# Opening of the up-projection: the fourth right-form difference made by GpSimd instead of VectorE

## The reference, cut to what matters

```
def conv_gated_mlp(h, w_up, conv_w, conv_b, w_down):
    """Up-projection -> causal depthwise conv (3) -> GELU-gated product -> down-projection."""
    z = causal_depthwise_conv(h @ w_up, conv_w, conv_b)
    g, val = jnp.split(z, 2, axis=-1)
    return (jax.nn.gelu(g, approximate=False) * val) @ w_down
```

## Time and profile before

| what | value |
|---|---|
| median of 3 runs | 2033.01 us (2030.88 to 2033.9) |
| the profiled execution's own time | 2032.3 us |
| its span | 2030.5 us |
| TensorE busy in the span | 1872.2 us, 92% |
| VectorE busy | 1555.6 us, 77% |
| GpSimd busy | 952.7 us, 47% |
| start of the up-projection in the span | 686.8 us |

### The profile page before, as it was taken

How to read it: one execution, slowest core, us unless ns; L and a number is a source line. 1 busy time by engine, 2 the same in 40 slices (tenths; PEclk the granted TensorE clock), 3 DMA queues, 4 the chain that set the end, 5 groups by cost and what they waited for, 6 DMA issues and landing times.

```text
span 2030.5 us, 27606 instructions
## 1 busy us (share of the span) xinstructions
PE 1872.2 (92%) x8520; PEld 1530.1 (75%) x8520; DVE 1555.6 (77%) x1876; ACT 977.4 (48%) x1508; POOL 952.7 (47%) x692
## 2 busy tenths in 40 slices
PE   4899999489999489999999799999999799999997
PEld 3788888367777367888888678888888588788886
DVE  8789878379998488877888988888888444666786
ACT  4565546367777344444444444444444333232454
POOL 5587788336665334444444344444443455620000
PEclk8999999689999689999999899999999899999999
DMA  7412111735443432322322322222224444487553
GB/s 252 145 36 73 62 62 47 193 103 149 139 145 109 170 123 91 116 92 102 116 92 102 119 94 103 103 103 104 103 103 149 149 147 147 122 275 235 176 187 136
DMA packets 200043, 257.48 MB, mean 127 GB/s; under 512 B 12208, under 2 KB 131504, under 8 KB 199472
## 3 DMA queue, kind: packets, MB, share of 16 engines
q1 hardware_dynamic: 191456, 233.24, 34.9%
q10 hardware_dynamic: 8528, 23.51, 3.2%
HBM read 172.10 MB, written 84.61 MB: 126 GB/s over the span
## 4 chain that ended last, share of the span: by engine, by line
PE 36%; issue 16%; POOL 7%; DVE 5%; DMA 2%; ACT 1%; POOLq 0%; SPq 0%; DVEq 0%; ACTq 0%
PE d_y L2300 18%; PE u_mm L2056 18%; POOL u_w_sum L1629 1%; POOL u_w_sum L1627 1%; DVE u_r_lo L1844 1%; POOL u_s L1643 1%; POOL u_s L1646 1%; POOL u_s L1640 1%; DMA d_wd_raw<-w_down 1%; DVE u_w_lo L1840 1%; DVE u_y L1875 1%; POOL d_wd_raw L2117 0%; DVE d_a_lo L1515 0%; POOL d_wd_raw L2115 0%; ACT u_r_hi L1696 0%
## 5 line engine op out<-in xcount | busy, mean ns | idle before, releaser
L2056 PE MATMUL u_mm<-u_r_hi,u_w_hi 128*128 128x512 f32 x1232 | 485.7, 394 | 43.8 <-DVE u_r_lo L1844 24.7
L2056 PE MATMUL u_mm<-u_r_lo,u_w_hi 128*128 128x512 f32 x1232 | 483.6, 393 | 0.0
L2056 PE MATMUL u_mm<-u_r_hi,u_w_lo 128*128 128x512 f32 x1232 | 483.5, 392 | 0.0
L2056 PEld LDWEIGHTS u_mm<-u_r_hi,u_w_hi 128*128 128x128 f32 x1232 | 233.9, 190 | 97.3 <-issue 43.9
L2056 PEld LDWEIGHTS u_mm<-u_r_hi,u_w_lo 128*128 128x128 f32 x1232 | 233.6, 190 | 49.3
L2056 PEld LDWEIGHTS u_mm<-u_r_lo,u_w_hi 128*128 128x128 f32 x1232 | 234.1, 190 | 48.1
L2300 PE MATMUL d_y<-d_wd_hi,d_a_hi 128*128 128x512 f32 x616 | 242.6, 394 | 18.4 <-DVE d_a_lo L1515 18.4
L2300 PE MATMUL d_y<-d_wd_lo,d_a_hi 128*128 128x512 f32 x616 | 241.8, 393 | 0.0
L2300 PE MATMUL d_y<-d_wd_hi,d_a_lo 128*128 128x512 f32 x616 | 241.5, 392 | 0.0
L1875 DVE SCALAR_TENSOR_TENSOR u_y<-u_z,u_taps,u_y 128x1024 f32<-128x1024 f32 x176 | 222.4, 1287 | 15.1 <-DVE u_z L1889 3.5
L524 DVE SCALAR_TENSOR_TENSOR a_acc<-a_glu,a_taps,a_acc 128x2048 f32<-128x2048 f32 x84 | 197.9, 2355 | 15.2 <-DVE a_acc L524 14.4
(11 more groups left out here) (214 smaller groups left out, 3470.0 us busy)
## 6 DMA issues: line engine op xcount, KB each, us to landing
u_w_raw<-w_up SPq DMA_DIRECT2D x44, 1024.0 KB, 5.0
d_a_raw<-gated_scr SPq DMA_DIRECT2D x56, 704.0 KB, 5.1
gated_scr<-u_s SPq DMA_DIRECT2D x88, 256.0 KB, 2.0
d_wd_raw<-w_down SPq DMA_DIRECT2D x88, 256.0 KB, 5.2
gated_scr<-u_gy SPq DMA_DIRECT2D x44, 256.0 KB, 2.1
a_xs<-x SPq DMA_DIRECT2D x16, 512.0 KB, 4.5
m_h_in<-h_scr SPq DMA_DIRECT2D x16, 512.0 KB, 4.0
h_scr<-m_r SPq DMA_DIRECT2D x16, 512.0 KB, 4.7
```

The source lines that it names most:

```text
L2056: last = nc.tensor.matmul(mm[BANK[s]][:], w[:, s, k, :], h[:, s, k, :], start=(s in FRESH and k == 0 and w is w_hi and h is r_hi), stop=(k ...
```

## The change

VectorE no longer makes t4. GpSimd makes it, with the same operands, between its first and second set of weight sums, once t2 is there and b21 has been read for the last time (the low part of Q2's right form). The wait of the second set for the low part of Q7's right form stays.

```diff
             left_sums(Step(0, 0, 0))
+            pool.wait_ge(t2_ok, 1)
+            pool.wait_ge(rlo_ok, FORMS[0].index(Q2) + 1)
+            nc.gpsimd.tensor_tensor(spare, spare, stage[:, 2, :, :], ALU.subtract).then_inc(t4_ok, 1)
             pool.wait_ge(rlo_ok, FORMS[0].index(Q7) + 1)
             left_sums(Step(0, 1, 0))
             step(Step(0, 1, 0))
...
                 nc.vector.tensor_tensor(stage[:, 0, :, :], stage[:, 2, :, :], stage[:, 0, :, :], ALU.subtract).then_inc(t3_ok, 1)
                 right_lo(0, Q6)
                 right_lo(0, Q7)
-                nc.vector.tensor_tensor(spare, spare, stage[:, 2, :, :], ALU.subtract).then_inc(t4_ok, 1)
                 make_u2(st)
                 make_u3(st)
                 make_c22(st)
```

## The result

Over 12 runs the changed kernel took 2037.57 us in the median (2035.83 to 2039.37), beside 2031.5 us for the kernel before in as many runs. The ratio is 1.0025 with a 95% interval of 1.0017 to 1.0033, which is 5.1 us slower, from 3.5 to 6.7. (The ratio is estimated over all runs: the two medians lie 6.1 us apart, the two means 5.4.) The profiled execution has a span of 2037.6 us. An unedited copy of the changed kernel gave 1.0027 (1.0018 to 1.0037) in another comparison, and an unedited copy of the kernel before gave 1.0005 (0.9996 to 1.0014).

The account below looks back on a forecast made before the run. TensorE, busy 92% of the span, bounds the kernel through holes in its stream; 0 (t4 off VectorE) + 0 (sums freed) + 4.4 (Q6's low part held) + 0 (clock) = +4.4 us, 2037.4 against the median, range 2035.0 to 2039.0.

Parts of the forecast that it names:

- The chain before Q6: VectorE's t2, t3 and Q6's low part, without a gap, set Q6's start; TensorE idled 4.44 us there.
- the hold of 4.4 us: GpSimd's t4 keeps VectorE from Q6's low part; Q6 starts at 724.8 instead of 720.44 us.
- Who goes first: After t2, t3 most likely runs first while GpSimd waits, then GpSimd's t4; either order makes Q6's low part equally late.
- Rival A: VectorE goes before GpSimd at both seams behind t3, 2033.0 us, or at one only, 2034.8; 8% for both.
- whoever has been waiting goes next: When VectorE and GpSimd want SBUF operands, one stands still for the other's instruction, then the waiting one goes.
- three cases: GpSimd sum or difference meeting VectorE at 700.56, 756.35 and 1119.34 us in the earlier trace; basis for the 4.4 us.
- The removal is worth nothing: VectorE loses t4's 2.28 us, but the next accumulation waited 0.86 us for TensorE anyway; worth 0.
- Nothing gives it back: Accumulations, Q3, Q4, second-half loads and all later steps shift with Q6; nothing later absorbs the 4.4 us.
- The clock: Slow matmuls after the hole before Q6 may number 8 to 14 instead of 11, -0.6 to +0.6 us; taken as zero.
- rival B's far case: Longer hole keeps TensorE at the lower clock through Q6 and Q7, 24 matmuls; about +7 us, 2040.0; rival's chance 6%.
- TensorE's idle time before Q6: Sign for the forecast in the changed kernel's trace: 8.8 us instead of 4.44 in the opening.
- the copy of 4.58 us: VectorE's 128x4 copy at 756.86 us beside a GpSimd difference, about 4.4 us over its usual 0.16; cited for the exclusive lock.

Follow-up runs that it names:

- extra difference: Kernel before, t4 still on VectorE, plus an unneeded 128x2048 GpSimd difference (t2 minus t1) where the changed kernel has t4; ratio to before 1.0031 (1.0019 to 1.0043).
- late difference: Changed kernel with GpSimd's t4 moved behind its wait for the low part of Q7's right form; ratio to before 1.0008 (0.9999 to 1.0017).
- quarters: Changed kernel with GpSimd's t4 cut into four instructions of 128x512; ratio to before 1.0010 (1.0001 to 1.0018).
- double: Changed kernel with a second, unneeded 128x2048 GpSimd difference right behind t4; ratio to before 1.0036 (1.0022 to 1.0050).
- kernel with t2 apart: Kernel before with t2 in memory of its own, made early, and Q3's low part moved behind those of Q6 and Q7; ratio 0.9983 (0.9974 to 0.9992).
- the memsets: Kernel before plus five GpSimd memsets of 128x1024 in a row, released by t2, t4 still on VectorE; ratio to before 1.000 (0.9991 to 1.0009).

## Why the prediction was right, point by point

- **The number:** +4.4 us forecast, +5.1 measured (3.5 to 6.7), so the size is right within the interval; whether it is above or below 0.2% the interval (0.17 to 0.33%) doesn't tell. That 2037.4 us was forecast and 2037.57 came out is in part luck: the kernel before had its median at 2031.5 us in 12 runs, 1.5 below the three runs that the sum started from.
- **The chain before Q6 and the hold of 4.4 us:** right. It was 4.30 us on VectorE, 4.31 us at Q6's start. The extra difference shows it without the move, the late difference shows the move without it.
- **Who goes first:** as forecast, t3 and then GpSimd's turn, although VectorE's next instruction was already taken up 0.09 us before t3's end. Rival A (VectorE keeps the path) is out for these seams: quarters and double hold VectorE at every seam at which GpSimd waits, and never for more than one instruction. As a rule, "whoever has been waiting goes next" is too strong: in the kernel with t2 apart VectorE kept the path at one seam (GpSimd's sum of 5.46 us). The prediction's three cases held none of that kind, so nothing in them told which kind this seam would be.
- **The removal is worth nothing:** right, and shown by the late difference: Q3 0.1 us earlier, the convolution 0.3 us later.
- **Nothing gives it back:** right to within what the runs tell. The opening is 4.8 to 5.0 us longer in two traces, the whole 5.1 and 5.5 us slower. The spans agree less well in their parts. The first traces differ by 7.1 us, the second by 5.3; up to t2 the changed kernel was 0.9 and 2.2 us faster in them, with nothing changed there, and from the convolution to the end it took 1294.5 and 1294.3 us beside 1291.6 and 1291.7 before. These 2.7 to 2.9 us behind the opening are not explained. They don't follow the hold: with the extra difference it was 1292.6 us, with two 1293.3, with the late one 1293.2. So that the opening and the whole agree so closely is in part chance.
- **The clock:** taken as zero, it was the one term that was mis-sized: +0.75 us between the first traces, just outside the 0.6 given for it, and +0.5 between the second, and more than 12 matmuls were slow, which I had named as a sign against me. Counted by their starts (0.43 us apart where slow, 0.23 where not), 15 and 13 matmuls of Q6 and Q7 were slow in the two traces of the changed kernel and 11 in both of before, a growth that goes with the 0.5 to 0.75 us. But with the same hole the extra difference gave 7, and Q5, with nothing changed before it, had 8, 12 and none. How much of it belongs to the longer hole stays open; rival B's far case (24 slow) did not appear.
- **A sign I named badly:** TensorE's idle time before Q6, forecast as 8.8 us, was 7.78 in one trace and 10.27 in the other, with Q6 at the same distance from t2. With the memsets it was 3.47, at the distance of before. It depends on when Q5 ended, so on the clock. The start of Q6 against t2 is the number to look at.
- **A row named for the wrong thing:** for the rule on VectorE with two SBUF inputs the prediction names the copy of 4.58 us as the agreeing trace, but that copy reads one. The row with two inputs is the low part of 4.82 us in the earlier trace rows; it agrees, and so do the low parts of the changed kernel.

## What to carry to other kernels

Before work goes from VectorE to GpSimd, look at what VectorE has in line at the moment at which GpSimd is released: if both engines' instructions read their two operands in SBUF, GpSimd can go in at the next seam (it did so at all such seams of the openings here but one), and the queue behind waits for its whole instruction, here 4.3 us to save an instruction of 2.3 us that nobody waited for. If it has to stand beside a critical chain, release it behind the chain (0.3 us in the opening here) or cut it into pieces (1.1 us before Q6). And first ask what the chain holds that isn't due yet: giving one difference its own memory took out a low part that stood in the way, and was worth 3.4 us.

## What the runs showed of the hardware

- Five memsets of GpSimd, 4.99 us, ran beside two-operand VectorE work with no delay on either side. VectorE's accumulations, with one operand in PSUM, took 0.69 us beside a GpSimd difference as without one. A VectorE copy of 128x4, which reads one operand in SBUF, was held all the same (4.58 us). The page "SBUF — State Buffer" of the Trainium skill, section "Who interferes with whom", says that VectorE with two SBUF inputs contends only with GpSimd instructions that read SBUF; the trace of the memsets agrees.
- When both engines wait, turns mostly alternate by instruction: 6.64 us for two low parts with four quarters waiting, 13.17 with two whole differences. One seam is an exception: a GpSimd sum of 1.3 us took 5.46, since two VectorE instructions ran in a row before it.
- After the same work and 3.5 us of idle time, Q5's 12 matmuls ran with 8 slow ones, with 12, or with none, in traces of kernels that don't differ up to there.
